# Block 2 of a two-block layer on one core: where x is added, where x is turned, and which engine splits which weights

## The chip, the cores and the metric

The kernel runs on one core of one Trainium2 chip. The time is the device time of one execution in microseconds. Engines are TensorE (PE in the profile, PEld for its weight loads), VectorE (DVE), ScalarE (ACT), GpSimd (POOL) and SyncE (SP), which issues the weight loads.

## What is computed

One sequence of 256 tokens with 1024 channels goes through two blocks, all in float32. Block 1 (attention, a gated convolution, a mixture of 32 experts) is not touched by the change. Block 2, cut to what matters:

```python
h = rms_norm_2(x, norm_mix_g)
z = h @ w_in            # q, f, i, g of the HGRN branch; q, k, v, forget logits of the FoX branch; two gates
y_a = hgrn2_mixer(...)  # kf = 1 - fg, decayed scores in chunks, rms_norm, silu(g)
y_b = forgetting_attention(q, k, v, f_logit, f_bias, q_gain, k_gain)   # q, k normed per head, cumulated log forget gate
x = x + (gate_a * (y_a @ w_branch_a) + gate_b * (y_b @ w_branch_b)) @ w_out
hf = rms_norm_2(x, norm_ffn_g)
x = x + (silu(hf @ w_ffn_gate) * (hf @ w_ffn_up)) @ w_ffn_down
hp = rms_norm_2(x, norm_ple_g)
x = x + sigmoid(hp @ w_ple_gate) * (p @ w_ple_proj)
```

## The kernel before, in words

**Split products.** A dense product of block 2 is done in three matmuls (`split`, L790 to L794): both operands are split into a lead, which is the operand rounded by a copy to the fast type, and a rest, operand minus lead; lead x lead, lead x rest and rest x lead are summed in PSUM. For the weights, each chunk of 512 columns (2 MB, 128 x 4096 in SBUF) is loaded by SyncE into a slot of a ring, copied to a lead by ScalarE (`lead_weights`, L1419, two halves of 2048), and the rest is made in place: the first half by VectorE (`rest_weights`, L1838, one instruction of 2048 columns), the second by GpSimd (L767, two of 1024). TensorE waits for the half, or on GpSimd's side the quarter, that the next k needs (`weights_ready`, L796).

**Order of the work.** Every engine has a hand-written order; there is no planner. TensorE goes through units: a unit is one chunk of weights for one tile of 128 tokens (`token_rows`, 8 k steps, 24 matmuls of 512 columns) or for two tiles of channels (`channel_tiles`, 48 matmuls of 256 columns). `UNITS2` gives them in the order fq, hf, hq, fk, fv, hi, hg, gate_b0 to gate_b3, two units each; then the branches pa_b and pb_b (L815), the output product wo_b (`out_rows`, L998), eleven ffn chunks, down, and the ple gate. Results go to PSUM through two rotations of four banks, `dense` and `small`; their order is fixed by `dense_order` and `small_order`, and a bank is claimed when the name four places back has been released. A lead has one of a few homes (`lead_home`, L625), and a new lead waits until TensorE is through with the chunk that held it (`lead_holds`, L636).

**Around the change, in block 2:**

- `fox_gate_logits` (L1183): after unit fq0, the forget logits, 2 token tiles x 8 k x 3 matmuls with the tokens as stationary operand and 8 columns; VectorE turns them to z, |z| and min(z, 0) (L2150 to L2154), then waits for both fq units and norms the queries (`head_norm`, L1775, 17 instructions); after that come the scaled keys hf0, the split of hq, and hf1 (L2161 to L2167). ScalarE computes exp and ln of the logits ahead of the exponential of hf0 (L1619 to L1623). The normed queries are turned after unit fk0 (L1261).
- The level loop (L2265 and on): for the crossing and seven levels of the HGRN scores VectorE makes differences (L2202 to L2210), ScalarE their exponential (`decay`, L1601), VectorE the decayed keys and queries (L2229, L2230), TensorE the scores (L1210, L1219), one level after each unit from fv0 on. In steps 1, 3, 5 and 7 VectorE also makes the rests of hi, hg, gate_b0 and gate_b1.
- After the branches: VectorE makes the rest of ffn0 and only then adds the four tiles of wo_b to x (L2335). TensorE turns x of the first token tile after the third wo_b unit and that of the second after the fourth (`norm_transposes`, L843 is the transpose). ScalarE makes the leads of the turned x (L1436) and its squares (L1428), VectorE the rests (L1871) and the row factors, for which ScalarE waits before it copies ffn1.
- At the end: VectorE makes the rests of ple0 and ple1, then adds the down products to x (L2370); TensorE turns x of the first tile ahead of the first ple unit, of the second ahead of the second. The four ple units are both column halves of the first token tile, then both of the second.

## Time and profile before

| | |
|---|---|
| runs | 1251.03, 1252.9, 1254.68 us, median 1252.9 |
| profiled execution | 1252.55 us, span of the trace 1250.7 us |
| TensorE | busy 1162.0 us of the span (93%), mean granted clock 0.974 |
| VectorE, ScalarE, GpSimd | 486.1, 414.2, 251.3 us |
| block 2 | from about 750 us to the end |

A row of the timeline gives start, duration, engine, line, operation, output<-inputs, shape and count, and in brackets the idle time of that engine ahead of it with what ended it. The name of a buffer is that of the tensor: `ring` holds the weights, `ring_r`, `gates_r`, `arena_r` are the same memory in the fast type. A PEclk of 1.00 is the 2.4 GHz level, 0.50 the 1.2 GHz level; values between are stretches with parts of both. A busy TensorE counts as busy at either.

### The profile page before, as it was taken

To read this page: it belongs to the slowest core of one execution; us is meant where nothing else is said; L and a number is where in the kernel's file an instruction comes from. 1 tells how busy PE (TensorE), PEld (TensorE's weight loads), DVE (VectorE), ACT (ScalarE), POOL (GpSimd) and SP (SyncE) were. 2 spreads that over 40 slices of the span, in tenths; PEclk is the share of its full clock that TensorE was granted. 3 is DMA by queue.
4 is the path that set the end of the run, shared out by engine and by line. 5 is a ranking of instruction groups with operands and counts; after the bars stand their busy time and mean duration, and the time that the engine had idled before them with its cause. 6 is when DMAs were issued, how large, how long until landed. Compare 5 with 4: busy or idle time off the path is not lost.

```text
span 1250.7 us, 15593 instructions
## 1 busy us (share of the span) xinstructions
PE 1162.0 (93%) x5920; PEld 786.0 (63%) x5920; DVE 486.1 (39%) x959; ACT 414.2 (33%) x608; POOL 251.3 (20%) x112
## 2 busy tenths in 40 slices
PE   4889999989999999999999988889999989999978
PEld 1659767764544454444444438878877778888856
DVE  2574552742222222222222215698444553333224
ACT  3524444231111111111111116644344264344332
POOL 0461233200000000000000003252214334443430
PEclk8989999989999999999999998989999999999988
DMA  9985366666999999999999991433114455555430
GB/s 376 359 270 214 137 228 243 270 268 269 363 423 421 422 423 420 422 423 421 422 422 422 422 402 62 150 135 134 68 68 144 135 192 159 187 168 202 168 135 34
DMA packets 89142, 331.63 MB, mean 265 GB/s; under 512 B 3825, under 2 KB 26642, under 8 KB 62466
## 3 DMA queue, kind: packets, MB, share of 16 engines
q1 hardware_dynamic: 88464, 330.36, 67.9%
q0 software_dynamic: 432, 0.48, 0.2%
q8 instruction: 37, 0.61, 0.2%
q14 instruction: 15, 0.12, 0.0%
q10 hardware_dynamic: 194, 0.06, 0.0%
HBM read 329.84 MB, written 1.05 MB: 265 GB/s over the span
## 4 chain that ended last, share of the span: by engine, by line
PE 67%; DMA 20%; DVE 6%; issue 2%; ACT 2%; SPq 1%; DVEq 0%; ACTq 0%
DMA ring<-in_w 16%; PE ps L792 12%; PE ps L1083 12%; PE ps L793 12%; PE ps L794 12%; PE ps L1128 5%; DMA ring<-in_w_ada 4%; PE ps L1070 3%; PE ps L852 1%; SPq L688 1%; PE ps L843 1%; DVE ring_r L1838 1%; ACT ring_r L1419 1%; PE ps L1219 1%; PE ps L906 1%
## 5 line engine op out<-in xcount | busy, mean ns | idle before, releaser
L767 POOL TENSOR_TENSOR ring_r<-ring,ring_r 128x1024 fp32r<-128x1024 f32 x88 | 227.1, 2601 | 890.6 <-ACT ring_r L1419 890.6
L1083 PE MATMUL ps<-ring,arena 128*64 128x512 f32 x1024 | 226.7, 595 | 8.5 <-DMA ring<-in_w 7.0
L793 PE MATMUL ps<-ring_r,hl_r 128*128 128x512 f32 x528 | 212.2, 402 | 0.0
L792 PE MATMUL ps<-ring_r,hl_r 128*128 128x512 f32 x480 | 198.2, 413 | 3.4 <-DVE hr_r L1918 2.5
L794 PE MATMUL ps<-ring_r,hr_r 128*128 128x512 f32 x480 | 192.6, 401 | 0.0
L1419 ACT ACTIVATE ring_r<-ring 128x2048 fp32r<-128x2048 f32 x90 | 167.1, 1905 | 69.8 <-PE ps L794 55.5
L1083 PEld LDWEIGHTS ps<-ring,arena 128*64 128x64 f32 x1024 | 75.0, 137 | 145.0 <-issue 129.4
L1838 DVE TENSOR_TENSOR ring_r<-ring,ring_r 128x2048 fp32r<-128x2048 f32 x46 | 109.9, 2389 | 101.6 <-ACT ring_r L1419 101.4
L1128 PE MATMUL ps<-ring,arena 128*64 128x512 f32 x480 | 108.0, 602 | 12.1 <-ACT arena L1569 10.9
L793 PEld LDWEIGHTS ps<-ring_r,hl_r 128*128 128x128 f32 x528 | 101.9, 193 | 22.4
L792 PEld LDWEIGHTS ps<-ring_r,hl_r 128*128 128x128 f32 x480 | 92.6, 193 | 31.1 <-issue 8.2
L794 PEld LDWEIGHTS ps<-ring_r,hr_r 128*128 128x128 f32 x480 | 92.3, 192 | 22.6
L1128 PEld LDWEIGHTS ps<-ring,arena 128*64 128x64 f32 x480 | 40.3, 138 | 69.5 <-issue 69.5
L1560 ACT ACTIVATE arena<-ps,mod,scale 128x128 f32<-128x128 f32 x64 | 24.1, 457 | 172.2 <-PE ps L1070 172.2
L1070 PEld LDWEIGHTS ps<-arena,ya 128*128 128x128 f32 x512 | 61.2, 199 | 14.0 <-issue 14.0
L1070 PE MATMUL ps<-arena,ya 128*128 128x128 f32 x512 | 64.3, 286 | 1.7 <-DVE flagf L2068 1.7
L1573 ACT ACTIVATE hl_r<-hl 128x512 fp32r<-128x512 f32 x32 | 20.2, 630 | 121.0 <-DVE hl L2114 121.0
L2114 DVE SCALAR_TENSOR_TENSOR hl<-ps,arena,ga2b 128x512 f32<-128x512 f32 x32 | 24.0, 751 | 83.5 <-PE ps L1128 83.5
L2100 DVE COPY arena<-ps 64x1 f32<-64x1 f32 x32 | 5.0, 157 | 125.1 <-PE ps L1097 124.6
L792 PE MATMUL ps<-hl_r,ring_r 128*128 128x256 f32 x160 | 46.9, 293 | 3.6 <-DVE ring_r L1838 3.6
L2107 DVE TENSOR_TENSOR arena<-arena,ps 128x512 f32<-128x512 f32 x16 | 11.0, 688 | 93.9 <-PE ps L1083 93.9
L794 PE MATMUL ps<-hl_r,ring_r 128*128 128x256 f32 x160 | 46.1, 288 | 0.0
(352 smaller groups left out, 1523.5 us busy)
## 6 DMA issues: line engine op xcount, KB each, us to landing
ring<-in_w SPq DMA_DIRECT2D x94, 2048.0 KB, 17.5
ring<-in_w_in SPq DMA_DIRECT2D x21, 2048.0 KB, 8.0
ring<-in_w_ada SPq DMA_DIRECT2D x8, 2048.0 KB, 9.8
ring<-in_w_ffn_gate SPq DMA_DIRECT2D x11, 1024.0 KB, 5.3
ring<-in_w_ffn_up SPq DMA_DIRECT2D x11, 1024.0 KB, 7.9
ring<-in_w_ffn_down SPq DMA_DIRECT2D x5, 2048.0 KB, 7.8
ring<-in_w_ada SPq DMA_DIRECT2D x8, 1024.0 KB, 11.9
ring<-in_w_o SPq DMA_DIRECT2D x2, 2048.0 KB, 7.8
```

Of the source, the lines that this page charges most:

```text
L767: nc.gpsimd.tensor_tensor(rest[:, a:b], w[:, a:b], lead[:, a:b].bitcast(F32), ALU.subtract).then_inc(sem("w_rest_b"), 1)
L792: mm(o, lhsT=a_lead, rhs=b_lead, start=start, stop=False, skip_group_check=True)
L793: mm(o, lhsT=a_lead, rhs=b_rest, start=False, stop=False, skip_group_check=True)
L794: return mm(o, lhsT=a_rest, rhs=b_lead, start=False, stop=stop, skip_group_check=True)
L1070: last = mm(G[:, j * P:(j + 1) * P], lhsT=xp[:, t, 4 * n + j, :], rhs=S[:, t, :], start=t == 0, stop=t == TT - 1)
L1083: last = mm(H[slots_of(e), :], lhsT=xs[:, k, slots_of(e)], rhs=wide(MOE_SLOT[2 * n + e])[:, k, :], start=k == 0, stop=k == KD - 1)
L1128: last = mm(Y[slots_of(e), :], lhsT=hidT[:, f, slots_of(e)], rhs=w2_rows(e, f, half, early), start=f == 0, stop=f == FT - 1)
L1419: af(lead, w, ACT.Copy).then_inc(sem("w_lead"), 1)
L1560: af(xs[:, k, :], GA[:, k * P:(k + 1) * P], ACT.Identity, scale=scale2[:, k:k + 1], bias=mod[:, 3 * KD + k:3 * KD + k + 1]).then_inc(sem(" ...
L1573: af(ys_l[:, cols_], ys[:, cols_], ACT.Copy).then_inc(sem("moe_ys_lead"), 1)
L1838: v.tensor_tensor(rest, w, lead.bitcast(F32), ALU.subtract).then_inc(sem("w_rest_a"), 1)
L2114: v.scalar_tensor_tensor(ys[:, cols_], Y, place_w, ga2b[:, cols_], ALU.mult, ALU.mult).then_inc(sem("moe_ys_scaled"), 1)
```

## The change

Five things in block 2. The forget logits are computed with the 8 weight columns as stationary operand and 256 tokens as columns, copied by ScalarE, and turned into token rows after fq1. The scaled keys and hq's rest go ahead of the query norm on VectorE, the turn of the queries goes from behind fk0 to behind fk1, and the logarithm of the logits joins that of the keys on ScalarE. Chunks fv, hi, hg and gate_b0 are split on VectorE in both halves, and not on GpSimd. The rest of ffn0 goes behind three of the adds to x, the turn of x's first tile into the third wo_b unit, of the second into the first ffn unit. At the end the adds to x and both tiles' rests go ahead of the rest of ple1, ScalarE copies ple1 behind the leads of the second tile, that tile is turned inside the first ple unit, and the ple units are both token tiles of the first column half, then both of the second, so that ple1's weights are wanted third and not second. Left out of the diff below: names and counts that follow from these (`foxr` in the bank orders, `PLE` for `WO` in the ple loops, merged semaphores).

```diff
@@ -360,10 +362,10 @@
             if name == "fq0":
-                small_order.append("fox")
+                small_order.append("foxr")
             if name == "fq1":
-                small_order.append("rsb")
-            if name == "fk0":
+                small_order += ["rsb", "fox"]
+            if name == "fk1":
                 small_order += ["tq_b0", "tq_b1"]
@@ -649,10 +653,15 @@
-        lead_done, rest_pool = [0], [0]
+        lead_done = [0]
         for m in range(len(split_chunks)):
             lead_done.append(lead_done[-1] + len(halves(m)))
-            rest_pool.append(rest_pool[-1] + 2 * (len(halves(m)) - 1))
+
+        ON_DVE = {M[name] for name in ("fv", "hi", "hg", "gate_b0")}
+        rest_dve, rest_pool = [0], [0]
+        for m in range(len(split_chunks)):
+            rest_dve.append(rest_dve[-1] + 1 + (m in ON_DVE))
+            rest_pool.append(rest_pool[-1] + (0 if m in ON_DVE else 2 * (len(halves(m)) - 1)))
@@ -795,8 +804,8 @@
-                if at < HALF_SLOT:
-                    pe.wait_ge(sem("w_rest_a"), m + 1)
+                if at < HALF_SLOT or m in ON_DVE:
+                    pe.wait_ge(sem("w_rest_a"), rest_dve[m] + 1 + (at >= HALF_SLOT))
                 else:
@@ -995,11 +1004,13 @@
-            def out_rows(tag, c, t):
+            def out_rows(tag, c, t, middle=None):
...
                 for k in range(KD):
+                    if k == KD // 2 and middle is not None:
+                        middle()
                     pe.wait_ge(sem("merged_rest"), 2 * t + k // 4 + 1 + 4 * SECOND[tag])
@@ -1181,13 +1192,21 @@
             def fox_gate_logits():
+
+                o = small.claim(pe, "foxr")
+                pe.wait_ge(sem("wfox_rest"), 1)
+                for k in range(KD):
+                    pe.wait_ge(*hm_ready(1, k))
+                    last = split(o[0:HEADS, 0:T], wf_lead[:, k, :], wf_rest[:, k, :], lead_h[:, k, :], rest_h[:, k, :],
+                                 k == 0, k == KD - 1)
+                last.then_inc(small.done, 1)
+
+            def fox_gate_columns():
                 o = small.claim(pe, "fox")
-                pe.wait_ge(sem("wfox_rest"), 1)
+                pe.wait_ge(sem("fox_rows"), 1)
                 for t in range(TT):
-                    for k in range(KD):
-                        pe.wait_ge(*hm_ready(t, k))
-                        last = split(o[:, t * HEADS:(t + 1) * HEADS], lead_h[:, k, t * P:(t + 1) * P],
-                                     rest_h[:, k, t * P:(t + 1) * P], wf_lead[:, k, :], wf_rest[:, k, :], k == 0, k == KD - 1)
+                    last = nc.tensor.transpose(o[:, t * HEADS:(t + 1) * HEADS], fox_rows[0:HEADS, t * P:(t + 1) * P],
+                                               ident[0:HEADS, 0:HEADS])
                 last.then_inc(small.done, 1)
@@ -1258,7 +1277,8 @@
                     token_factors()
-                if name == "fk0":
+                    fox_gate_columns()
+                if name == "fk1":
                     head_transposes("tq_b", qrow, "q_normed", 2)
@@ -1288,10 +1308,8 @@
             out_rows("_b", 1, 0)
-            out_rows("_b", 0, 1)
-            norm_transposes("xf", x3_ready, TH[0:2])
+            out_rows("_b", 0, 1, lambda: norm_transposes("xf", x3_ready, TH[0:2]))
             out_rows("_b", 1, 1)
-            norm_transposes("xf", x3_ready, TH[2:4])
@@ -1304,7 +1322,8 @@
                 for t in range(TT):
-                    token_rows(f"ffn{m}{t}", f"ffn{m}", t, lambda t, k: (sem("norm_rest"), TT * KD + KD * t + k + 1))
+                    middle = None if (m, t) != (0, 0) else lambda: norm_transposes("xf", x3_ready, TH[2:4])
+                    token_rows(f"ffn{m}{t}", f"ffn{m}", t, lambda t, k: (sem("norm_rest"), TT * KD + KD * t + k + 1), middle)
                     if t == 0 and m == FFN_CHUNKS - 1:
@@ -1359,10 +1378,9 @@
             norm_transposes("xp", x4_ready, TH[0:2])
-            for n, (c, t) in enumerate(WO):
-                if n == 1:
-                    norm_transposes("xp", x4_ready, TH[2:4])
-                token_rows(f"ple{c}{t}", f"ple{c}", t, lambda t, k: (sem("norm_rest"), 2 * TT * KD + KD * t + k + 1))
+            for n, (c, t) in enumerate(PLE):
+                middle = None if n else lambda: norm_transposes("xp", x4_ready, TH[2:4])
+                token_rows(f"ple{c}{t}", f"ple{c}", t, lambda t, k: (sem("norm_rest"), 2 * TT * KD + KD * t + k + 1), middle)
@@ -1607,6 +1625,8 @@
                 if unit == "fq0":
+                    src = small.ready(act_, "foxr")
+                    af(fox_rows[0:HEADS, :], src[0:HEADS, 0:T], ACT.Copy).then_inc(sem("fox_rows"), 1)
                     act_.wait_ge(sem("rs_ready"), 1)
@@ -1616,14 +1636,14 @@
                         act_.wait_ge(sem("fox_abs_ready"), 1)
-                        af(fz[:, 2, :], fz[:, 1, :], ACT.Exp, scale=-1.0).then_inc(sem("fox_exp_ready"), 1)
-                        act_.wait_ge(sem("fox_exp_ready"), 1)
-                        af(fz[:, 2, :], fz[:, 2, :], ACT.Ln, bias=1.0).then_inc(sem("fox_ln_ready"), 1)
+                        af(fz[:, 2, :], fz[:, 1, :], ACT.Exp, scale=-1.0).then_inc(sem("fox_exp_ln"), 1)
                     act_.wait_ge(sem("hf_scaled"), u + 1)
...
                         af(khT, khT, ACT.Ln, bias=1.0).then_inc(sem("hf_ln"), 1)
+                        act_.wait_ge(sem("fox_exp_ln"), 1)
+                        af(fz[:, 2, :], fz[:, 2, :], ACT.Ln, bias=1.0).then_inc(sem("fox_exp_ln"), 1)
                         act_.wait_ge(sem("hf_ln"), 1)
@@ -1642,10 +1662,9 @@
                     af(rsb, src[:, 0:T], ACT.Copy).then_inc(sem("rsb_ready"), 1)
-                if unit == "fk0":
+                if unit == "fk1":
                     for i in range(2):
                         copy_out(two_tiles(qT, i), small, f"tq_b{i}", "qT_ready")
-                if unit == "fk1":
                     decay(0)
@@ -1676,13 +1695,13 @@
+            square(0, 0, 3, x3_ready)
+            norm_leads("xf", "norm_ffn_g_2", TH[0:2])
+            square(0, 1, 3, x3_ready)
             lead_weights(M["ffn0"])
-            square(0, 0, 3, x3_ready)
-            square(0, 1, 3, x3_ready)
-            norm_leads("xf", "norm_ffn_g_2", TH[0:2])
             square(1, 0, 3, x3_ready)
+            norm_leads("xf", "norm_ffn_g_2", TH[2:4])
             square(1, 1, 3, x3_ready)
-            norm_leads("xf", "norm_ffn_g_2", TH[2:4])
@@ -1709,7 +1728,6 @@
             lead_weights(M["ple0"])
-            lead_weights(M["ple1"])
@@ -1718,10 +1736,11 @@
             norm_leads("xp", "norm_ple_g_2", TH[2:4])
+            lead_weights(M["ple1"])
             square(1, 0, 4, x4_ready)
...
             act_.wait_ge(sem("rs_ready"), 4)
-            for n, (c, t) in enumerate(WO):
+            for n, (c, t) in enumerate(PLE):
                 src = dense.ready(act_, f"ple{c}{t}")
@@ -1833,9 +1852,10 @@
-                w, rest, lead = halves(m)[0]
-                dve.wait_ge(sem("w_lead"), lead_done[m] + 1)
-                v.tensor_tensor(rest, w, lead.bitcast(F32), ALU.subtract).then_inc(sem("w_rest_a"), 1)
+                for n in range(2 if m in ON_DVE else 1):
+                    w, rest, lead = halves(m)[n]
+                    dve.wait_ge(sem("w_lead"), lead_done[m] + 1 + n)
+                    v.tensor_tensor(rest, w, lead.bitcast(F32), ALU.subtract).then_inc(sem("w_rest_a"), 1)
@@ -2152,8 +2172,6 @@
             link(v.tensor_scalar(fz[:, 0, :], fz[:, 3, :], 0.0, None, ALU.min))
-            dve.wait_ge(*rows_ready("fq", 1))
-            head_norm(qrow, 2, False, "q_normed")
@@ -2161,10 +2179,12 @@
+            rest_weights(M["hq"])
             hf_scaled(0)
-            rest_weights(M["hq"])
             hf_scaled(1)
-            dve.wait_ge(sem("fox_ln_ready"), 1)
+            dve.wait_ge(*rows_ready("fq", 1))
+            head_norm(qrow, 2, False, "q_normed")
+            dve.wait_ge(sem("fox_exp_ln"), 2)
             link(v.tensor_tensor(fz[:, 0, :], fz[:, 0, :], fz[:, 2, :], ALU.subtract))
@@ -2328,13 +2348,14 @@
             merged_rests("_b", 1)
-            rest_weights(M["ffn0"])
             for n, (c, t) in enumerate(WO):
...
                 v.scalar_tensor_tensor(into, src, 0.5, into, ALU.mult, ALU.add).then_inc(sem("x3_ready"), 1)
+                if n == 1:
+                    norm_rests(1, "xf", "norm_ffn_g_2", 0)
                 if n == 2:
-                    norm_rests(1, "xf", "norm_ffn_g_2", 0)
+                    rest_weights(M["ffn0"])
             norm_rests(1, "xf", "norm_ffn_g_2", 1)
@@ -2363,17 +2384,16 @@
                 rest_weights(m)
-            rest_weights(M["ple1"])
             for n, (t, h) in enumerate(TH):
...
                 v.tensor_tensor(into, into, src, ALU.add).then_inc(sem("x4_ready"), 1)
-                if n == 1:
-                    norm_rests(2, "xp", "norm_ple_g_2", 0)
+            norm_rests(2, "xp", "norm_ple_g_2", 0)
             norm_rests(2, "xp", "norm_ple_g_2", 1)
+            rest_weights(M["ple1"])
             row_factors(4, 6)
             v.tensor_scalar(rs[:, 7, :], rs[:, 6, :], 0.5, None, ALU.mult).then_inc(sem("rs_ready"), 1)
-            for n, (c, t) in enumerate(WO):
+            for n, (c, t) in enumerate(PLE):
                 dve.wait_ge(sem("ple_tanh"), n + 1)
```

## Rows read from the trace of the kernel before

**Rows 1.** Waits of TensorE from 740 us on: waiter, releaser, us in total, times, longest

```profile
PE ps L843 <- DVE x L2370: 7.1, 1, 7.1
...
PE ps L843 <- DVE x L2335: 5.6, 2, 5.3
...
PE ps L1219 <- DVE ring L2230: 3.9, 2, 2.8
...
PE ps L792 <- DVE ring_r L1838: 3.6, 1, 3.6
...
PE ps L1210 <- DVE ring L2230: 1.5, 1, 1.5
```

**Rows 2.** TensorE by stretches: us, busy (instructions), granted clock, DMA share, GB/s

```profile
763.30:768.63 5.33, 5.33 (x49) 0.99 0.00 0
...
768.63:775.80 7.17, 7.17 (x25) 0.77 0.00 0
...
775.80:787.95 12.15, 12.14 (x101) 1.00 0.49 174
...
791.50:804.60 13.10, 13.08 (x97) 0.87 0.27 102
...
830.80:860.20 29.40, 25.57 (x120) 0.88 0.40 143
...
860.20:998.95 138.75, 137.49 (x704) 1.00 0.31 108
...
998.95:1013.60 14.65, 9.04 (x40) 0.88 0.45 144
...
1013.60:1209.95 196.35, 196.35 (x867) 1.00 0.54 179
...
1209.95:1246.10 36.15, 28.21 (x112) 0.81 0.11 39
```

**Rows 3.** Timelines of VectorE, ScalarE and GpSimd between 776 and 820 us

```profile
776.82 1.23 DVE L1780 TENSOR_TENSOR sp<-arena 128x1024 f32<-128x1024 f32 x1 [7.29 <-ACT arena L1409]
...
789.10 2.28 DVE L1838 TENSOR_TENSOR ring_r<-ring,ring_r 128x2048 fp32r<-128x2048 f32 x1
...
810.54 3.70 ACT L1419 ACTIVATE ring_r<-ring 128x2048 fp32r<-128x2048 f32 x2
...
814.32 5.51 POOL L767 TENSOR_TENSOR ring_r<-ring,ring_r 128x1024 fp32r<-128x1024 f32 x2 [7.85 <-ACT ring_r L1419]
...
814.68 5.70 DVE L2192 SCALAR_TENSOR_TENSOR ring<-gates,ring 128x512 f32<-128x512 f32 x2
```

**Rows 4.** Source view of line 2210: minimum, median and maximum in ns

```profile
L2210 DVE TENSOR_TENSOR ya<-uy x7: 678/684/2857, 822.0 to 868.3; 128x512 f32<-128x512 f32 x7
```

**Rows 5.** Timelines around the output product, 999 to 1024 us

```profile
999.43 3.71 ACT L1419 ACTIVATE ring_r<-ring 128x2048 fp32r<-128x2048 f32 x2 [10.89 <-PE ps L794]
...
1012.47 0.69 DVE L2335 SCALAR_TENSOR_TENSOR x<-ps,x 128x512 f32<-128x512 f32 x1 [3.32 <-PE ps L794]
...
1013.22 0.66 PE L843 MATMUL ps<-cst,x 128*128 128x128 f32 x4 [0.35 <-DVE x L2335]
...
1019.90 3.72 ACT L1419 ACTIVATE ring_r<-ring 128x2048 fp32r<-128x2048 f32 x2 [3.91 <-DVE rs L2340]
...
1021.85 2.29 DVE L1838 TENSOR_TENSOR ring_r<-ring,ring_r 128x2048 fp32r<-128x2048 f32 x1 [1.98 <-ACT ring_r L1419]
```

**Rows 6.** Timelines ahead of the ple units, 1206 to 1220 us

```profile
1206.37 2.29 DVE L1838 TENSOR_TENSOR ring_r<-ring,ring_r 128x2048 fp32r<-128x2048 f32 x1 [8.95 <-ACT ring_r L1419]
...
1212.12 3.71 ACT L1419 ACTIVATE gates_r<-ring 128x2048 fp32r<-128x2048 f32 x2 [3.97 <-DMA ring<-in_w_ple_gate]
...
1215.90 4.99 POOL L767 TENSOR_TENSOR ring_r<-ring,gates_r 128x1024 fp32r<-128x1024 f32 x2 [2.70 <-ACT gates_r L1419]
...
1216.27 1.28 DVE L2370 TENSOR_TENSOR x<-x,ps 128x512 f32<-128x512 f32 x2
...
1218.15 2.17 ACT L1436 ACTIVATE hl_r<-ps,pcol 128x128 fp32r<-128x128 f32 x8 [2.33 <-PE ps L843]
```

18 lines of the change are left out of this document (11 added, 7 removed).

## Prediction

> **What bounds the kernel now.** I read the page first, then the waits of TensorE, then a table of its busy time and granted clock by stretches, and last the timelines of the other engines around each gap. TensorE is busy for most of the span, so a change pays only where it idles, runs at 1.2 GHz, or does matmuls that could be fewer. The change touches only block 2, which starts near 750 us. TensorE's five large waits there [rows 1] are all for VectorE: 7.1 before the last transposes, 5.6 before those ahead of the feed-forward part, 3.9 and 1.5 for the decayed queries of the levels, 3.6 for the split of hq's weights, 21.7 us together. The stretches [rows 2] show what hangs on them. From 860.2 to 998.95 and from 1013.6 to 1209.95 TensorE is full at the full clock: there nothing can be won, and whatever is won ahead of them is kept. Around the gaps the granted clock is 0.77 to 0.88, so each gap costs again in slow matmuls. One wide matmul (128x512) takes 0.233 us at full clock (the 196.35 us stretch holds 816 of them and some 50 short ones of 0.11), a unit of 24 takes 5.6. Matmuls of 256 columns take 0.12 (12.15 us for 96 and four short ones).
>
> **Part 1: forget logits as rows.** Before: 48 matmuls of 8 columns in 5.33 us, 0.111 each, since each brings its own 128x128 weights; and fq1 behind them took 7.17 us at clock 0.77 where 5.6 is normal [rows 2]. After: 24 matmuls of 256 columns, 24 x 0.12 = 2.9 us, and two small transposes behind fq1, 0.2. Gain 5.33 - 3.1 = 2.2. The dense stream should keep the clock, gain 1.55. ScalarE gets one small copy; it stands idle for most of fq1. Bounds: 1.5 if the clock still drops, 3.8 if not; I take 3.75.
> The Trainium skill ("TensorE: Matmul & The Clock Gate", Back-to-back issue gap) gives 262 cycles for 256 columns, 0.109 us; by that the rows would cost 2.6 and not 2.9 us, 0.3 less. The trace's 0.12 decides.
>
> **Part 2: keys scaled and hq split ahead of the query norm.** VectorE began the norm at 776.8 and reached hq's split at 789.1 [rows 3], so TensorE stood 3.55 us and then ran hq at clock 0.87, 13.1 us where 96 x 0.12 = 11.5 is normal [rows 2]. After: hq's split waits only for ScalarE's lead copy, which follows fq1 directly, so it is done some 6 us before hq starts. Gain 3.55 + 1.5 = 5.1. The query transposes move from behind fk0 to behind fk1, same count. What is late next: the norm. It moves behind the second scaled key tile and pushes the gate chain (sigmoid, log, scan, scaled queries). Before, fv's lead copy, which stands at the end of that chain on ScalarE, began at 810.54, that is 22.6 us after TensorE's end of hf1 (787.95). I keep 22.4 us: the norm's 7.5 us come in, hq's 2.3 us split goes out, the 2.3 us delays in the norm go, ScalarE saves two table loads. Up to hf1 the gain of part 1 holds, so fv's first split half ends at 26.6 us (22.4 + 1.9 + 2.3) after hf1, while TensorE could start fv0 after 11.5 + 11.2 + 0.8 = 23.5. A new stall of 3.1 us; bounds 0 and 6 (the chain shorter or longer by 3).
>
> **Part 3: fv, hi, hg, gate_b0 split on VectorE alone.** The row that matters: VectorE's subtraction L2210 takes 684 ns in the median and 2857 at worst [rows 4], and L2192, two instructions while GpSimd split fv from 814.3 to 819.8, took 5.70 us [rows 3]; such an instruction is 0.69 alone. Adds that read PSUM are not stretched: 1.28 for two beside GpSimd's 4.99 [rows 6]. So a GpSimd pair holds VectorE for about 4.3 us, and the VectorE half that replaces it costs 2.29: net 2.0 for each of four chunks, 8 us of VectorE time between 810 and 865, where it has hardly a pause.
> The Trainium skill ("SBUF — State Buffer", Who interferes with whom) says that a VectorE instruction with two SBUF inputs and a GpSimd instruction that reads SBUF exclude each other for the whole instruction; by it fk's split, still on GpSimd, would hold the scan or fk's own half of VectorE. The trace agrees (5.70). The sum stays as it is.
> After fv's first half, its second takes 2.3, and what follows up to the first level took 9.2 (814.8 to 824.0) with 4.3 of stretch: 26.6 + 2.3 + 9.2 - 4.3 = 33.8 after hf1, against fv0's end at 32.2. A gap of 1.6, then by the same counting 0.4 and 0.3 at the levels behind. Before, the levels lost 1.5 + 2.75 + 1.15 = 5.4 in gaps, and 830.8 to 860.2 ran at clock 0.88: 29.4 x 0.12 = 3.4 at half clock lost. Now 3.1 + 1.6 + 0.7 = 5.4. Net gain 3.4. A stall of 2.75 us was followed by a slow stretch, those of 1.15 to 1.5 were not, so I take off 1.3 for the 3.1 us one. Front total 3.75 + 5.1 + 3.4 - 1.3 = 11.0.
>
> **Part 4: x ahead of ffn0's split.** Before, VectorE held x behind ffn0's split, whose lead copy could start only when wo_b0 had been read (999.43) [rows 5]; TensorE stood 5.3 us, and then ran slow: 998.95 to 1013.6 holds 24 wide matmuls and 16 transposes, 14.65 us where 5.6 + 1.6 is enough. After, the transposes lie inside units: ffn0's first unit starts at 998.95 + 0.8 + 5.6 = 1005.35, with the second transposes 0.8 inside it: 7.4 earlier. ffn0's split (lead half 1.9, VectorE's half 2.3 [rows 5]) ends at 999.43 + 1.9 + 2.3 + 0.5 = 1004.1, in time. But x's last add is now at 1005.4 instead of 1012.47, its transposes wait for half a unit (1008.1), and ScalarE still waits for the row factors before ffn1's lead copy. Before, from the last transposes (1013.2) to that copy (1019.9) it took 6.7, and 4.2 more to the split's end (1024.14): 1008.1 + 6.6 + 4.2 = 1018.9, and TensorE wants ffn1 at 1005.35 + 12.0 = 1017.35. A new gap of 1.6, with 0.3 for GpSimd's half: gain 7.4 - 1.9 = 5.5. Bounds 3.5 (clock falls in the gap) and 7.4 (no gap).
>
> **Part 5: x ahead of ple1's split, ple units in order of tokens.** Before, the adds (1216.27) stood behind ple1's split, whose weights landed at 1212.12 [rows 6]; TensorE had ended at 1209.95. The stretch 1209.95 to 1246.1 is 36.15 us for 96 wide matmuls and 16 transposes: 22.4 + 1.7 = 24.1 at full clock, so 12.0 are lost. After: the first adds follow ple0's split, 1208.7; transposes 1209.8 to 1210.8; ScalarE's lead copies (8 in 2.17) and VectorE's remainders let ple00 start near 1212.3, a gap of 1.5. The rest runs through: ple1's lead copies follow those of t=1 near 1217.8, its splits end near 1222, and ple10, now third, begins at 1224.2. Left of the 12.0 is a loss of 1.5 to 2.4, gain 9.6 to 10.5; I take 9.7. Bounds 6 (all of ple00 at half clock, another 1.5 of waiting) and 11. The tail behind the last matmul, 4.6 us, stays.
>
> **Edits at nothing:** the merged semaphores, and ScalarE's reordered squares, covered by its idle time in the units; without it a square costs some 0.9 us (estimate, from eight copies of 128 columns in 2.17 [rows 6]). DMA: SP's weight loads keep their order and their releases (last unit of each chunk), and each chunk still has the 11.7 us of two units to land in; the output pieces go out in the new order, the last one alone at the end as before.
>
> **Sum.** 11.0 + 5.5 + 9.7 = 26.2. The profiled execution took 1252.55 (span 1250.7), within 0.4 of the median 1252.9: 1252.55 - 26.2 = 1226.4, rounded to 1226.5.
>
> **Rivals.**
> VectorE's chain becomes the bound of the front: the fv stall is 6 us and each level stays a little late. For it: no pauses there, four more halves, the norm moved into the gate chain. Against: 8 us of stretch go. The front gains 3 to 5, and with it the end or middle 2 less: 1233 to 1237. Chance 0.17.
> The clock: all new gaps (3.1, 1.6, 1.6, 1.5) are followed by slow stretches of 1.6 us each: 1231 to 1233 if the rest holds; it is for me the upper part of the forecast.
> The gaps close better than I count (norm chain shorter, no slow stretch): 4 + 2 + 1 more, 1215 to 1221. Chance 0.14.
> Slower: in the level loop VectorE now waits for ScalarE's second lead half of hi and hg, while ScalarE's next exponential waits for VectorE's difference behind that split. If each of the 7 levels came late by over 3.8 us, 26 us would be lost, and the time be 1256 to 1260. Against it: the exponential in question belongs to a difference issued before the split, and ScalarE idles over 4 us per unit there. Chance 0.04. That the edits don't act, or cancel within 0.3% (3.8 us, about what a measurement of this kernel can tell from no change), 0.03.
> The forecast itself, 1221 to 1233: 0.62. Faster 0.93, same 0.03, slower 0.04. The range 1219 to 1237 leaves out less than 0.2: its upper end is the sum with the lower bounds of two parts, its lower end with the upper bounds of all.
>
> **What would show it.** In the profile after: 24 matmuls at the logits in 2.9 us and a full clock in fq1; no wait before hq; a wait before fv0 of about 3; VectorE's L2192 and level lines near 0.69; the first feed-forward unit some 18 us earlier than now, a small wait at ffn1; under 2 us between the down projection and ple00. If the waits at fv and the levels exceed 8 us, or the clock falls behind each gap, the forecast is wrong at that step.

## The result and the profile after

The change made the kernel faster: 1225.2 us in the median of four runs (1222.15 to 1226.13) against 1252.7 for four runs of the kernel before beside them, ratio 0.9776 (95% interval 0.9753 to 0.9798). The profiled execution took 1225.39 us with a span of 1223.5. Its page begins:

```profile
span 1223.5 us, 15545 instructions
...
PE 1149.6 (94%) x5898; PEld 775.7 (63%) x5898; DVE 479.5 (39%) x963; ACT 411.3 (34%) x607; POOL 230.3 (19%) x104
```

TensorE has 12.4 us less of busy time (1162.0 before), GpSimd 21.0 less, and VectorE, which took over four halves, has 6.6 us less too (486.1 before): what it gained in unhindered instructions is more than what it took over. In the kernel after, lines stand some 10 to 20 lower: the three matmuls are L801 to L803, the transposes L852, ScalarE's lead copy L1437, VectorE's rest L1858, GpSimd's rest L776, the decayed keys and queries L2249 and L2250.

TensorE's waits from 740 us on, which answer to [rows 1]:

```profile
PE ps L801 <- DVE ring_r L1858: 5.5, 2, 3.5
PE ps L852 <- issue: 5.2, 1, 5.2
PE ps L801 <- issue: 1.3, 1, 1.3
...
PE ps L801 <- POOL ring_r L776: 0.2, 1, 0.2
```

Of the five large waits for VectorE (21.7 us) one kind is left, 5.5 us for L1858: 3.46 before fk0 and 2.01 before ffn1. The 1.3 is the gap ahead of the first ple unit. The 5.2 ahead of the first transposes of block 2 has no named releaser; it is not the change's (more on it at the end). Both waits before transposes of x (7.1 and 5.6) and all those at the levels are gone.

TensorE's busy time and granted clock by stretches, which answer to [rows 2]:

```profile
763.27:766.00 2.73, 2.73 (x26) 1.00 0.00 0
766.00:771.62 5.62, 5.62 (x26) 1.00 0.00 0
...
772.37:784.10 11.73, 11.73 (x99) 1.00 0.51 180
784.10:795.67 11.57, 11.57 (x97) 1.00 0.51 183
795.67:799.13 3.46, 0.00 (x1) 0.89 0.66 211
799.13:813.20 14.07, 14.07 (x48) 0.78 0.26 98
...
1193.17:1218.90 25.73, 24.42 (x112) 1.00 0.14 52
```

The gaps and slow stretches of before have closed or shrunk: logits and fq1 at 1.00, hf and hq dense, and the last stretch takes 25.73 where it took 36.15. One is new: 3.46 us without work before fk0, and behind it 14.07 us at a mean clock of 0.78. The timelines of VectorE and GpSimd there, which answer to [rows 3]:

```profile
774.68 2.29 DVE L1858 TENSOR_TENSOR ring_r<-ring,ring_r 128x2048 fp32r<-128x2048 f32 x1 [1.54 <-ACT ring_r L1437]
...
784.80 1.22 DVE L1799 TENSOR_TENSOR sp<-arena 128x1024 f32<-128x1024 f32 x1
...
792.51 1.38 DVE L2194 TENSOR_SCALAR gates<-gates,lbt 128x256 f32<-128x256 f32 x4
...
794.53 4.45 DVE L1858 TENSOR_TENSOR ring_r<-ring,ring_r 128x2048 fp32r<-128x2048 f32 x1
798.90 4.80 DVE L2201 TENSOR_TENSOR_SCAN uy<-cst,gates 128x128 f32<-128x128 f32 x8
...
811.94 1.41 DVE L2212 SCALAR_TENSOR_TENSOR ring<-gates,ring 128x512 f32<-128x512 f32 x2
```

```profile
794.08 7.13 POOL L776 TENSOR_TENSOR ring_r<-ring,ring_r 128x1024 fp32r<-128x1024 f32 x2 [12.49 <-ACT ring_r L1437]
```

hq's rest (774.68) is done 7 us before hq starts. The norm (from 784.80) is dense and ends at 792.3. But fk's rest stands behind the norm and the gates: it begins at 794.53, only 1.1 us before TensorE wants it, and takes 4.45 instead of 2.29, for GpSimd works on the other half of fk at the same time (7.13 for two pieces). The scan behind it is held as well: its first instruction takes 2.59, the other seven 0.39 each. L2212, which stood beside fv's split and took 5.70 before, now takes 1.41. The level lines show the same in the source view of L2230, which answers to [rows 4]:

```profile
L2230 DVE TENSOR_TENSOR ya<-uy x7: 683/686/687, 814.9 to 856.6; 128x512 f32<-128x512 f32 x7
```

No instance is stretched any more; the longest was 2857 ns. Around the output product, answering to [rows 5], and ahead of the ple units, answering to [rows 6]:

```profile
993.62 0.69 DVE L2354 SCALAR_TENSOR_TENSOR x<-ps,x 128x512 f32<-128x512 f32 x1 [1.25 <-PE ps L803]
...
1003.32 3.71 ACT L1437 ACTIVATE ring_r<-ring 128x2048 fp32r<-128x2048 f32 x2 [3.66 <-DVE rs L2361]
...
1005.26 2.29 DVE L1858 TENSOR_TENSOR ring_r<-ring,ring_r 128x2048 fp32r<-128x2048 f32 x1 [1.98 <-ACT ring_r L1437]
...
1007.70 0.47 PE L801 MATMUL ps<-ring_r,hl_r 128*128 128x512 f32 x1 [2.01 <-DVE ring_r L1858]
...
1191.80 2.48 DVE L2390 TENSOR_TENSOR x<-x,ps 128x512 f32<-128x512 f32 x4
1193.64 2.17 ACT L1454 ACTIVATE hl_r<-ps,pcol 128x128 fp32r<-128x128 f32 x8 [2.28 <-PE ps L852]
...
1195.33 0.47 PE L801 MATMUL ps<-ring_r,hl_r 128*128 128x512 f32 x1 [1.29 <-issue]
```

ScalarE's lead copy for ffn1 (1003.32) still waits for the row factors (`rs`), and from it to TensorE's start are 4.4 us, of which 2.01 are a gap. At the end the adds (1191.80) are followed by the leads (1193.64), and ple00 starts 1.29 after the last transposes.

**A measure by stages.** The runs below are compared by three stretches, each from TensorE's own events: the front, from block 2's first transposes of x to the fifth of the seven levels, behind which TensorE is dense; the middle, from there to the end of the down products; the end, from there to the last matmul. Before they took 114.84, 341.38 and 36.18 us; after 102.25, 336.51 and 25.71. That is 12.6 + 4.9 + 10.5 = 28.0 won, of which 0.7 is given back by a later start of block 2: 27.3, and the spans differ by 27.2.

The front begins with work that neither the change nor any run touches, the first transposes and unit fq0. Up to the first matmul of the logits they took 9.57 us before, at a mean granted clock of 0.76, and 8.86 after, at 0.83; over all the traces 8.9 to 10.2. So 0.7 of the 12.6 is not the change's. From the logits to the fifth level it took 105.3 us before and 93.4 after, 11.9 less. The table has this shorter stretch beside the front, and it is the better measure of what a run does there.

### The profile page after: what moved, and what is told of

The parts are those of the page before. It is cut to its first block, busy times and chain, and to the rows that moved or that the text cites. A ratio compares the mean times of both kernels' runs of the same rounds, so it can differ in the third digit from the quotient of the medians.

```text
span 1223.5 us, 15545 instructions
## 1 busy us (share of the span) xinstructions
PE 1149.6 (94%) x5898; PEld 775.7 (63%) x5898; DVE 479.5 (39%) x963; ACT 411.3 (34%) x607; POOL 230.3 (19%) x104
## 4 chain that ended last, share of the span: by engine, by line
PE 74%; DMA 17%; DVE 3%; issue 2%; ACT 1%; SPq 1%; POOL 0%; DVEq 0%; ACTq 0%
DMA ring<-in_w 14%; PE ps L801 14%; PE ps L802 13%; PE ps L803 13%; PE ps L1094 13%; PE ps L1139 5%; DMA ring<-in_w_ada 3%; PE ps L1081 3%; PE ps L861 2%; PE ps L1238 1%; SPq L697 1%; PE ps L915 1%; PE ps L913 1%; PE ps L852 1%; DVE ring_r L1858 1%
## 5 line engine op out<-in xcount | busy, mean ns | idle before, releaser
L776 POOL TENSOR_TENSOR ring_r<-ring,ring_r 128x1024 fp32r<-128x1024 f32 x80 | 206.1, 2597 | 895.6 <-ACT ring_r L1437 895.6
L801 PE MATMUL ps<-ring_r,hl_r 128*128 128x512 f32 x480 | 197.2, 411 | 9.1 <-DVE ring_r L1858 5.5
L803 PE MATMUL ps<-ring_r,hr_r 128*128 128x512 f32 x480 | 192.0, 400 | 0.0
L1437 ACT ACTIVATE ring_r<-ring 128x2048 fp32r<-128x2048 f32 x90 | 167.2, 1907 | 60.8 <-PE ps L803 45.0
L1858 DVE TENSOR_TENSOR ring_r<-ring,ring_r 128x2048 fp32r<-128x2048 f32 x50 | 118.4, 2374 | 92.4 <-ACT ring_r L1437 92.2
L801 PEld LDWEIGHTS ps<-ring_r,hl_r 128*128 128x128 f32 x480 | 91.7, 191 | 37.4 <-issue 15.0
L803 PEld LDWEIGHTS ps<-ring_r,hr_r 128*128 128x128 f32 x480 | 91.7, 191 | 22.4
L801 PE MATMUL ps<-hl_r,ring_r 128*128 128x256 f32 x160 | 45.9, 287 | 0.0
L802 PE MATMUL ps<-hr_r,ring_r 128*128 128x256 f32 x160 | 45.1, 282 | 0.0
## 6 DMA issues: line engine op xcount, KB each, us to landing
ring<-in_w_ada SPq DMA_DIRECT2D x8, 1024.0 KB, 12.4
```

Of the source, the lines that this page charges most:

```text
L776: nc.gpsimd.tensor_tensor(rest[:, a:b], w[:, a:b], lead[:, a:b].bitcast(F32), ALU.subtract).then_inc(sem("w_rest_b"), 1)
L801: mm(o, lhsT=a_lead, rhs=b_lead, start=start, stop=False, skip_group_check=True)
L802: mm(o, lhsT=a_lead, rhs=b_rest, start=False, stop=False, skip_group_check=True)
L803: return mm(o, lhsT=a_rest, rhs=b_lead, start=False, stop=stop, skip_group_check=True)
L1437: af(lead, w, ACT.Copy).then_inc(sem("w_lead"), 1)
L1858: v.tensor_tensor(rest, w, lead.bitcast(F32), ALU.subtract).then_inc(sem("w_rest_a"), 1)
```

## The experiments

Each line of a diff stands for its hunk in the change. In the table are the median, the ratio to the kernel before on the same chip and its 95% interval, and, from the profiled execution, the three stages in us and the front counted from the logits on.

| run | median us | ratio | front | from the logits | middle | end |
|---|---|---|---|---|---|---|
| before | 1252.7 | | 114.8 | 105.3 | 341.4 | 36.2 |
| after | 1225.2 | 0.9776 [0.9753, 0.9798] | 102.3 | 93.4 | 336.5 | 25.7 |
| e1 front order and logits | 1245.7 | 0.9939 [0.9921, 0.9957] | 109.5 | 100.4 | 341.7 | 34.9 |
| e2 splits on VectorE | 1245.3 | 0.9931 [0.9905, 0.9958] | 105.9 | 96.5 | 342.4 | 34.9 |
| e3 middle | 1245.8 | 0.9940 [0.9915, 0.9964] | 114.9 | 105.6 | 336.2 | 35.1 |
| e4 end | 1242.1 | 0.9908 [0.9877, 0.9940] | 115.8 | 106.9 | 341.9 | 25.7 |
| e5 after, no split on VectorE | 1231.6 | 0.9822 [0.9798, 0.9846] | 109.4 | 100.4 | 336.2 | 25.7 |
| e6 after, fk on VectorE too | 1222.0 | 0.9742 [0.9716, 0.9768] | 98.5 | 89.5 | 336.2 | 25.7 |
| e7 after, fk's rest earlier | 1226.0 | 0.9777 [0.9753, 0.9801] | 103.0 | 93.1 | 337.6 | 25.7 |
| e8 after, ffn1's lead earlier | 1222.0 | 0.9746 [0.9722, 0.9770] | 102.4 | 92.2 | 334.4 | 25.7 |
| e9 logits as rows alone | 1248.3 | 0.9962 [0.9946, 0.9977] | 112.0 | 101.8 | 341.6 | 34.9 |
| e10 order of the front alone | 1252.0 | 0.9994 [0.9982, 1.0006] | 115.3 | 105.8 | 341.0 | 36.1 |
| e11 e6 and e8 together | 1219.6 | 0.9726 [0.9712, 0.9740] | 98.9 | 89.5 | 334.1 | 25.7 |
| e12 e11, fk's halves apart | 1220.3 | 0.9735 [0.9720, 0.9750] | 98.6 | 89.5 | 334.1 | 25.7 |

A stage that a run does not touch stays within 1.1 us (front, middle), 1.6 us (from the logits) and 1.3 us (end). The cause is how long the clock stays at the 1.2 GHz level behind a wait, which differs between traces of the same instructions. The unchanged end took 36.2 and 36.1 us in the kernel before and e10, and 34.9 to 35.1 in e1, e2, e3 and e9.

### One part of the change at a time

**e1_front**: the kernel before with parts 1 and 2 alone.

```diff
-                small_order.append("fox")
+                small_order.append("foxr")
...
+            rest_weights(M["hq"])
             hf_scaled(0)
-            rest_weights(M["hq"])
             hf_scaled(1)
+            dve.wait_ge(*rows_ready("fq", 1))
+            head_norm(qrow, 2, False, "q_normed")
+            dve.wait_ge(sem("fox_exp_ln"), 2)
```

> The kernel before with the forget logits as rows and the query norm behind the scaled keys, and nothing else of the change. Theory A (each stall is the end of one chain, and the parts add up to the 27 us): 3.8 us from the logits and 5.1 from hq, less a wait of about 3.5 before fk0 with a slow stretch of 2.9 behind it, and the levels still stretched by GpSimd: 2 to 5 us faster, 1248 to 1251. Theory B (the new wait before fk0 only uses up slack that the level loop would lose anyway): 8 to 9 us faster, 1244.

The front is 5.4 us shorter, from the logits on 4.9. Its waits in the front:

```profile
PE ps L1228 <- DVE ring L2241: 3.9, 2, 2.8
...
PE ps L793 <- DVE ring_r L1849: 3.5, 1, 3.5
```

The 3.5 is before fk0, and the two waits at levels stand as before, 3.9 with 2.8 the longest; the 1.5 at the crossing fell to 0.6. So these two parts win what they were to win until hq has ended, and give back about 5 at once, 3.5 in the new wait and 1.5 in slow matmuls behind it.

**e2_dve**: the kernel before with part 3 alone.

```diff
+        ON_DVE = {M[name] for name in ("fv", "hi", "hg", "gate_b0")}
...
-                if len(halves(m)) == 2:
+                if len(halves(m)) == 2 and m not in ON_DVE:
...
+                for n in range(2 if m in ON_DVE else 1):
+                    w, rest, lead = halves(m)[n]
+                    dve.wait_ge(sem("w_lead"), lead_done[m] + 1 + n)
```

> The kernel before with fv, hi, hg and gate_b0 split on VectorE in both halves, and nothing else. Theory A (GpSimd holds two-input instructions of VectorE for longer than its half would cost there): VectorE's lines of the level loop fall to 0.69 us each, the 2.8 us wait at the levels goes with the slow stretch behind it, 6 to 8 us faster, 1245 to 1247. Theory B (the level loop is bound by VectorE's own work, and four more halves of 2.3 us add to it): same or up to 5 us slower.

The front is 8.9 us shorter (8.8 from the logits on), the most that any part wins there. Its waits and the source view of the line that [rows 4] showed:

```profile
PE ps L797 <- DVE ring_r L1844: 3.6, 1, 3.6
...
PE ps L1224 <- DVE ring L2236: 0.3, 1, 0.3
```

```profile
L2216 DVE TENSOR_TENSOR ya<-uy x7: 684/685/687, 817.8 to 857.5; 128x512 f32<-128x512 f32 x7
```

The wait before hq is the old one, the waits at the levels fell from 3.9 to 0.3, the 1.5 at the crossing went, and no instance of this line is stretched. That VectorE does more work itself did not make it late.

**e3_mid** and **e4_end**: parts 4 and 5 alone, each on the kernel before.

```diff
-            rest_weights(M["ffn0"])
...
                 if n == 2:
-                    norm_rests(1, "xf", "norm_ffn_g_2", 0)
+                    rest_weights(M["ffn0"])
```

> The kernel before with x added ahead of ffn0's split and turned inside the units, and nothing else. Theory A: the 5.3 us wait and the slow stretch behind it go, 7.4 us, and a wait of 2.0 before ffn1 comes, since ScalarE still waits for the row factors before it copies ffn1: 5.0 us faster, 1247.6. Theory B (parts depend on each other): without the earlier front the wait before ffn1 has another length, and the gain is under 3 or over 7.

```diff
-            rest_weights(M["ple1"])
...
             norm_rests(2, "xp", "norm_ple_g_2", 1)
+            rest_weights(M["ple1"])
...
-            for n, (c, t) in enumerate(WO):
+            for n, (c, t) in enumerate(PLE):
```

> The kernel before with x added ahead of ple1's split and the ple units in the new order, and nothing else. Theory A: the 7.1 us wait goes but for 1.3, and the half-clock stretch behind it wholly, 10.3 us faster, 1242.4. Theory B (the clock would come back as late as before, since a gap remains): 6 to 7 us faster.

The middle of e3 is 5.2 us shorter, the end of e4 10.5. One line of e3 from 900 to 1150 us, and one of e4:

```profile
PE ps L792 <- DVE ring_r L1839: 1.7, 1, 1.7
```

```profile
PE ps L795 <- issue: 1.3, 1, 1.3
```

Each shows the small new gap that the whole change shows too (1.7 here and 2.0 there before ffn1, 1.3 both times before ple00), so both parts are independent of the front and of each other. Stage by stage the four parts alone give 5.4 + 8.9 + 5.2 + 10.5 = 30.0; the whole gives 28.0. Of the 2.0, 1.7 are lost in the front, where parts 1 and 2 with part 3 bring 12.6 and not 14.3 (from the logits 11.9 and not 13.7). Of that, 1.2 is no more than a longer slow stretch in the one trace of the kernel after: e8 has the same instructions and the same wait there, and takes 92.2 from the logits on and not 93.4. The four ratios alone say 7.6 + 8.6 + 7.5 + 11.5 = 35 us, against 28 for the whole; their intervals together leave some 7 us either way, so the medians do not contradict the stages, and are too coarse to show that the parts add up.

**e9_logits** and **e10_order** cut the first two parts once more: the logits as rows alone (with one merged semaphore, so that the new one finds room), and the new order on VectorE, TensorE and ScalarE alone.

```diff
+                for k in range(KD):
+                    pe.wait_ge(*hm_ready(1, k))
+                    last = split(o[0:HEADS, 0:T], wf_lead[:, k, :], wf_rest[:, k, :], lead_h[:, k, :], rest_h[:, k, :],
+                                 k == 0, k == KD - 1)
```

> The kernel before with the forget logits as rows (and one merged semaphore) and nothing else. From the first transposes of block 2 to the fifth of the seven levels the kernel before takes 114.8 us, the changed one 102.3. Theory A (fewer matmuls and the clock kept in fq1 are worth their 3.8 us at once, since what follows is bound by TensorE up to hq): the logits and fq1 take 8.4 us in place of 12.5, and 3.8 us are left at the fifth level, 111.0. Theory B (VectorE's query norm, which starts when fq1 ends, moves with it, but hq's split and the levels wait for VectorE, so that part is lost in longer waits): 1 to 2.5 us left.

The front is 2.9 shorter, from the logits on 3.4. Logits and fq1 ran nearly as in the whole change:

```profile
763.07:765.88 2.81, 2.81 (x26) 1.00 0.00 0
765.88:772.04 6.16, 6.16 (x30) 1.00 0.00 0
```

2.81 + 6.16 = 8.97 where [rows 2] had 12.50. Up to the first matmul of hf 3.7 us are won. From there to the crossing 0.3 is lost: the wait before hq is 3.8, where it was 3.6, and the slow stretch behind it is longer, but the crossing waits 0.8 and not 1.5. Behind the crossing nothing is lost (44.6 us both times). So the gain lies between the two values expected, nearer the first.

```diff
+            rest_weights(M["hq"])
             hf_scaled(0)
-            rest_weights(M["hq"])
             hf_scaled(1)
```

> The kernel before with the scaled keys and hq's split ahead of the query norm, the query transposes behind fk1 and the joined logarithms, and nothing else. Both parts of the front together left 5.4 us at the fifth level (109.5 in place of 114.8). Theory A (the order moves a wait more than it removes one): the wait of 3.6 before hq and its slow stretch go, 5.1, a wait of 3.5 before fk0 with a slow stretch comes, and 1 to 2 us are left: 113 to 114. Theory B (order and logits are worth the same): 4 to 5 us left, 110.

```profile
PE ps L792 <- DVE ring_r L1837: 3.5, 1, 3.5
```

The ratio is 0.9994, the front 0.5 longer. The wait of 3.6 before hq is gone and one of 3.5 stands before fk0; its rest L1837 began at 797.73 and took 4.46. But the stages tell more than the total. From the first matmul of hf to the crossing the order wins 1.1 us (46.7 for 47.8). From there to the fifth level it took 46.2 and not 44.6, since here the clock fell to 0.50 behind the wait of 1.14 us at a level, a wait that stands in the kernel before, e1, e4, e5 and e9 too and was followed by no slow matmul there. So the order alone is worth about 1 us, too little for the ten runs to show (their interval goes from 2.3 us faster to 0.8 slower). With the rows in place it is worth 1.5 (from the logits, e1 100.4 against e9 101.8); the 2.5 by which the two fronts differ is for the rest the clock ahead of the logits.

### What is left in the changed kernel

**e5_pool**: the kernel after, all rests shared with GpSimd as before.

```diff
-        ON_DVE = {M[name] for name in ("fv", "hi", "hg", "gate_b0")}
+        ON_DVE = set()
```

> The changed kernel with fv, hi, hg and gate_b0 split half on GpSimd again. Theory A (the exclusion by GpSimd costs VectorE some 8 us net between fv and gate_b0): VectorE's two-input lines go back to 2 to 3 us where GpSimd works, waits come back at the levels, 5 to 8 us slower than the changed kernel, 1230 to 1233. Theory B (after the reordering the level loop has slack enough): within 1.5 us of 1225.

6.4 us slower in the median, the front 7.2 longer (7.0 from the logits on, which is e1's time to 0.1 us). The two waits at the levels are back to the digit, and so nearly is the stretched instance, 2862 ns for 2857; at the crossing it waits 0.6, as in e1, and not 1.5:

```profile
PE ps L801 <- DVE ring_r L1858: 5.1, 2, 3.5
...
PE ps L1238 <- DVE ring L2250: 3.9, 2, 2.8
```

```profile
L2230 DVE TENSOR_TENSOR ya<-uy x7: 677/685/2862, 818.8 to 865.1; 128x512 f32<-128x512 f32 x7
```

**e6_fk_dve**: fk as well on VectorE alone.

```diff
-        ON_DVE = {M[name] for name in ("fv", "hi", "hg", "gate_b0")}
+        ON_DVE = {M[name] for name in ("fk", "fv", "hi", "hg", "gate_b0")}
```

> The changed kernel with fk split wholly on VectorE too. Theory A (the 3.46 us wait before fk0 is 2.2 us of GpSimd's hold on VectorE's half, 4.45 us where 2.29 is normal): that half ends 2.2 us earlier, the wait falls to 1.3, the slow stretch of 2.9 us behind it goes, but the second half (2.3 us) stands where two holds of some 2.2 us stood: 3 to 5 us faster, 1220 to 1222. Theory B (the wait is the moved norm's length and GpSimd has no part): the wait stays over 3, same time.

The front is another 3.8 us shorter. VectorE around fk, and TensorE's stretch over its wait and most of fk's two units:

```profile
795.98 4.49 DVE L1858 TENSOR_TENSOR ring_r<-ring,ring_r 128x2048 fp32r<-128x2048 f32 x2
800.38 2.63 DVE L2201 TENSOR_TENSOR_SCAN uy<-cst,gates 128x128 f32<-128x128 f32 x8
```

```profile
797.10:809.00 11.90, 10.61 (x46) 1.00 0.51 177
```

Both halves of fk take 4.49 together, what one half took beside GpSimd (4.45). TensorE may start after the first of them, so its wait (11.90 - 10.61 = 1.29) is 2.2 shorter, and the clock is 1.00 behind it, which saves the 2.9 us lost in slow matmuls. A wait of 0.6 is new at a level; behind the crossing 0.9 in all is given back. The scan takes 2.63, not 4.80.

**e7_fk_first**: fk's rest right behind the norm, ahead of the forget gates.

```diff
             head_norm(qrow, 2, False, "q_normed")
+            rest_weights(M["fk"])
             dve.wait_ge(sem("fox_exp_ln"), 2)
...
-            rest_weights(M["fk"])
             dve.wait_ge(sem("logf_ready"), 1)
```

> The changed kernel with VectorE's half of fk's split moved ahead of the forget gates and of the 2.1 us of gate work, directly behind the query norm. Theory A (the wait before fk0 comes from the place of this half in VectorE's order): the half ends at 794.5 us, before fk0 is due at 795.7, so the wait of 3.46 and the 2.9 us of slow matmuls behind it go; the gate chain is 2.3 us later, and part of it comes back as a wait of 2 to 3 before fv0: 2 to 4 us faster, 1221 to 1223. Theory B (whatever is won at fk0 comes back at fv0 and the levels): same within 1 us.

No gain in the median (1226.0 for 1225.2). The front is 0.7 longer by the clock ahead of the logits, and from the logits on 0.3 shorter. The wait did not go, it moved from fk0 to fv0:

```profile
PE ps L801 <- DVE ring_r L1858: 5.4, 2, 3.4
```

GpSimd and VectorE show why:

```profile
795.93 5.05 POOL L776 TENSOR_TENSOR ring_r<-ring,ring_r 128x1024 fp32r<-128x1024 f32 x2 [12.50 <-ACT ring_r L1437]
```

```profile
794.08 2.29 DVE L1858 TENSOR_TENSOR ring_r<-ring,ring_r 128x2048 fp32r<-128x2048 f32 x1
796.29 2.38 DVE L2189 TENSOR_TENSOR fz<-fz 128x16 f32<-128x16 f32 x1
798.71 2.31 DVE L2190 TENSOR_SCALAR fz<-fz 128x16 f32<-128x16 f32 x1
```

The rest itself is now undisturbed (2.29), but two instructions of 16 columns, 0.17 each in the kernel after, take 2.38 and 2.31: one for each piece of GpSimd. The gate chain is 4.4 us later for it. Counted from the first matmul of hf, fv's lead copy begins 1.2 us later than in the kernel after, where GpSimd held fk's rest and the scan in place of these two.

**e8_ffn1**: ScalarE makes ffn1's lead before it waits for the row factors.

```diff
-            act_.wait_ge(sem("rs_ready"), 3)
             for m in range(FFN_CHUNKS):
                 lead_weights(M["ffn0"] + m + 1)
+                if m == 0:
+                    act_.wait_ge(sem("rs_ready"), 3)
```

> The changed kernel with ScalarE's lead copy of ffn1 ahead of its wait for the row factors. Theory A: the copy then runs ahead of the factors, VectorE's half follows them directly, and the 2.01 us wait before ffn1 falls to below 0.5, and the 0.18 us one goes: 1.7 us faster, 1223.5. Theory B (the factors or GpSimd's half set that wait): same.

The middle is 2.1 us shorter and the wait of 2.01 before ffn1 is gone (GpSimd's 0.2 stays). The median fell by 3.2; in the trace 1.2 of it is the shorter slow stretch behind fk0, which the edit does not touch.

**e11_both** joins e6 and e8, **e12_best** also sets fk's first half ahead of the forget gates and its second at the old place (the second argument of `rest_weights` in its diff names the halves).

> The changed kernel with fk split wholly on VectorE and ffn1 copied ahead of the wait for the row factors. Theory A (the two stand at different places and add up): 3.7 us less to the fifth level and 2.1 less behind it, 5.8 us faster than the changed kernel, 1219.4. Theory B (they don't add): 1222, as with either.

The two add up: 1219.6 us, 5.6 less than the change and 33 less than the kernel before. Of the waits for rests one is left, before fk0; beside it stands 0.6 at a level, as in e6:

```profile
PE ps L801 <- DVE ring_r L1859: 1.3, 1, 1.3
```

```diff
+            rest_weights(M["fk"], (0,))
             dve.wait_ge(sem("fox_exp_ln"), 2)
...
-            rest_weights(M["fk"])
+            rest_weights(M["fk"], (1,))
             dve.wait_ge(sem("logf_ready"), 1)
```

> As the kernel with both, and VectorE's first half of fk's split ahead of the forget gates, its second half left behind them. Theory A (the scan waited for VectorE's own order and not for the gates, so the first half can go ahead at no cost once GpSimd is out): the wait of 1.3 before fk0 goes and none comes before fv0, 1.3 us less than the kernel with both. Theory B (as when this half was moved with GpSimd still in it, the wait turns up again before fv0): no less.

```profile
PE ps L801 <- DVE ring_r L1859: 0.7, 1, 0.7
PE ps L1238 <- DVE ring L2252: 0.6, 1, 0.6
PE ps L1229 <- DVE ring L2252: 0.5, 1, 0.5
```

The 1.3 before fk0 became 0.7 inside it, for the second half, and 0.5 came up at the crossing; the 0.6 at a level is e11's too. From the logits on both take 89.5 us, and the medians cannot be told apart. The version to keep is e11.

## Why the prediction was right, step by step

The forecast was a gain of 26.2 us against the profiled execution; it was 27.2. The terms were 11.0, 5.5 and 9.7, the stages show 12.6, 4.9 and 10.5. The front's own gain is 11.9, for 0.7 of the 12.6 lie ahead of the logits, and are cancelled by the later start of 0.7.

**Part 1** (3.75) came out against this trace of the kernel before. From the logits to the first matmul of hf it took 12.9 us before (763.30 to 776.19) and 9.1 after (763.27 to 772.37), 3.8 less. The logits took 2.73, a little under the 2.9 of the sum, and fq1 ran at 1.00. The 0.12 for a matmul of 256 columns was from a stretch where each matmul brings 128 columns of weights; here, with 8, it was 0.114. What the old form loses behind the logits varies: with the same instructions e3 and e4 took 14.5 us for the stretch that took 12.9 in the kernel before, e2 and e10, so part 1 is worth 3.8 to 5.4 from trace to trace.

**Part 2** (5.1 up to the end of hq) came out: from the first matmul of hf to the end of hq it took 28.4 us before (776.19 to 804.60) and 23.3 after (772.37 to 795.67). What the step had wrong is the place of what is late next. The prediction put a new stall of 3.1 us at fv0; it came at fk0, 3.46. I had followed the moved norm into the gate chain and as far as fv's lead copy, and had not asked when the next rest on VectorE's own queue, fk's, would come: it stands behind the same norm. e10 shows that this is the price of the order by itself. The chain to fv0 was sized well in total: the first half of fv's rest ended 25.7 us after hf1 (807.53 + 2.29 against 784.10), and the forecast was 26.6. In part that is luck: 4.3 us of the 25.7 are holds by GpSimd at fk (4.45 for 2.29, 4.80 for 2.63), while the time of the kernel before from which the forecast starts has 2.6 of them (its scan took 5.24). So 1.7 us of holding were not counted, and the rest of the chain was 2.6 shorter than counted. e7 shows the forecast place: with fk's rest out of the way the wait stands at fv0 with 3.4. In the whole change the later start of fv0 covers that wait, for fk0's wait and slow stretch come first, and delay TensorE by 6.4 (5.1 in e8, and no wait at fv0 there either); the two are the same lateness of VectorE, met at its first or at its second place.

**The clock behind it** was mis-sized for this trace: 1.3 was taken off, and the 14.07 us from 799.13 hold 48 wide matmuls, which need 48 x 0.233 = 11.2, so 2.9 were lost. The trace shows 0.50 from 799 to 805:

```profile
799.00:801.00 2.00, 1.87 (x5) 0.50 1.05 409
...
803.00:805.00 2.00, 2.00 (x6) 0.50 0.00 0
805.00:807.00 2.00, 2.00 (x10) 0.95 0.02 4
```

The same 48 matmuls behind the same wait (3.46 to 3.48) are in four more traces. In e8, which has the same instructions around it:

```profile
799.52:812.38 12.86, 12.86 (x49) 0.87 0.29 110
```

That is 1.7 lost, and in e1, e5 and e10 (12.65, 12.69 and 12.73 us) 1.5. So 1.3 is near what the wait costs in four traces of five, and the kernel after's own profile drew the longer stretch.

**Part 3** (net 3.4 from hq's end to the levels) was undersized, and in this trace the clock took back most of that. Until the crossing TensorE gave back 4.6 (its lead of 8.9 at hq's end is 4.3 at the crossing, 819.70 against 823.99): 6.4 in the wait and the slow stretch, less the 1.5 that it had waited at the crossing before, and some tenths. Then it won 7.6 up to the fifth level (37.0 us against 44.6), with no gap at all where the sum had 1.6 at the crossing and 0.7 at levels. So the new gaps were 3.5 and not 5.4, 1.9 better, the clock 1.6 worse; and the old loss behind hq was 9.3 in this measure, where the sum had 5.4 + 3.4 = 8.8 (0.1 of the difference is a slip, 29.4 x 0.12 is 3.5). Together parts 1 to 3 gave 3.8 + 5.1 + 3.0 = 11.9. The price of a chunk was right (5.70 fell to 1.41; both halves of a rest take 4.49). The unsafe step was to add the gaps at the crossing and the levels to the one ahead of them: where TensorE has stood 3.5 us and run slow for a while, VectorE is in time for what follows, in the whole change, in e7 and in e8. This holds only while nothing delays VectorE anew: e1 and e5 wait 3.5 at fk0 and then 0.6 at the crossing and 3.9 at the levels, where GpSimd still holds it.

e2 and e5 give 8.8 and 7.0 for part 3 from the logits on, alone and taken out; 1.2 of the difference is the slow stretch behind fk0. The Trainium skill ("SBUF — State Buffer", Who interferes with whom) says that a VectorE instruction with two SBUF inputs contends with a GpSimd instruction that reads SBUF, and that the one that starts first gets the shared ports for the whole instruction. The traces agree for fk's half (4.45), the first instruction of the scan (2.59 for 0.39) and, in e7, an instruction of 16 columns (2.38). I had named the scan and fk's own half as the ones that this would hold, and left the sum as it was; that is a term that was missing. The 3.8 us that e6 wins in the front are its price, 2.2 of the wait and the slow stretch behind it, less what comes back at the levels.

**Part 4** (5.5) came out at 4.9, by the wait that was named, 2.01 and not 1.6 before ffn1, and 0.2 of GpSimd. Its reason, ScalarE held by the row factors ahead of a copy that does not need them, is shown by e8: 2.1.

**Part 5** (9.7, bounds 6 and 11) came out at 10.5. The gap was 1.29, predicted 1.5, and no slow stretch followed it, where the sum had kept up to 0.9 of loss beyond the gap. The base is a long one: against the 34.9 to 35.1 us that the old end took in four other traces the new one wins 9.2.

**The rivals.** That VectorE's chain becomes the bound was the right mechanism at one place (fk0) and stopped there; at the levels, where it was to go on, VectorE was early. That all four new gaps draw a slow stretch did not happen: one of them did, though in e7 the gap before ffn1 did too. That level units wait for ScalarE's second lead half did not happen, no wait at hi or hg is in any run. Of the third rival, gaps that close better, the levels are an example. The front's total is as near as it is because two errors, 1.9 for the gaps and 1.6 for the clock, had opposite signs in the trace that was compared; the middle and the end were right by their own steps. Of the signs named, the wait before fv0 is the one that did not come; it stood at fk0.

## What to carry to other kernels

When an item moves in front of others on an in-order queue, list everything behind it in that queue with the time at which its user wants it, and not only the chain that starts from it. Work shared by halves between VectorE and GpSimd costs VectorE more than the half that it saves, if VectorE has anything else to do then: here one instruction for each piece of GpSimd was held to the piece's end, however small. A late engine is late once, unless something delays it again: do not add its waits at successive places, look for the first, and for what would make it late anew. And before a difference of 1 or 2 us between two traces is given to an edit, compare the stretches that the edit does not touch, and those that ran at the 1.2 GHz level.
